# First layer of a two-layer backbone: context tokens in a pass of their own, latents' up projection as seven block products

## The reference

```python
D_MODEL = 1024; SEQ = 1024; CTX_LEN = 256; DEPTH = 2; D_FF = 2816

def _modulate(x, shift, scale):
    return x * (1 + scale) + shift

def _conv_ffn(u, w_up, conv_w, w_down):
    gate, val = jnp.split(_dwconv3(u @ w_up, conv_w), 2, axis=-1)
    return (jax.nn.silu(gate) * val) @ w_down

# per layer, after the first residual h = h + gt1 * mixer(...)
h = h + gt2 * _conv_ffn(_modulate(_rmsnorm(h, norm2[layer]), sh2, sc2), *ffn)
if not last:
    hc = hc + cgt2 * _conv_ffn(_modulate(_rmsnorm(hc, norm2[layer]), csh2, csc2), *ffn)
```

## Time and profile before

| what | value |
|---|---|
| median of 3 runs | 3210.61 us (3210.31 to 3213.64) |
| profiled execution | 3206.37 us |
| its span in the trace | 3204.4 us |
| mean granted clock of TensorE | 0.97 |
| busy: TensorE, VectorE, ACT, POOL | 3016.6, 1765.9, 953.6, 1015.6 us |
| read from and written to HBM | 185.5 MB, 20.8 MB |

### The profile page before, as it was taken

The page is one execution under the profiler, slowest core; times in us unless marked ns, Lnnn a source line. Parts: engine busy times, 40 slices in busy tenths (PEclk is TensorE's granted clock), DMA queues, the critical chain, the costliest instruction groups (busy, mean ns, idle before and its releaser), DMA issues. The chain is left out here.

```text
span 3204.4 us, 67073 instructions
## 1 busy us (share of the span) xinstructions
PE 3016.6 (94%) x28758; PEld 2470.4 (77%) x28758; DVE 1765.9 (55%) x2673; ACT 953.6 (30%) x1800; POOL 1015.6 (32%) x644
## 2 busy tenths in 40 slices
PE   6998999999999999899989889999988899999999
PEld 4655888888888888788867667878767678888887
DVE  4623444555554454722246666777755766666666
ACT  4011221000000000220036566666632433233232
POOL 3212223223333323152311100000004466666664
PEclk9998999999999999999989989999989999999999
DMA  5431011222222221022312011111012111111112
GB/s 236 151 123 37 23 46 46 86 92 92 92 92 92 80 85 40 20 89 81 99 47 63 21 33 29 31 32 34 23 40 92 38 42 66 40 53 66 40 53 79
DMA packets 86541, 210.55 MB, mean 66 GB/s; under 512 B 8434, under 2 KB 44658, under 8 KB 86003
## 3 DMA queue, kind: packets, MB, share of 16 engines
q1 hardware_dynamic: 73442, 157.21, 14.7%
q10 hardware_dynamic: 12816, 49.16, 4.4%
HBM read 185.50 MB, written 20.84 MB: 64 GB/s over the span
## 5 line engine op out<-in xcount | busy, mean ns | idle before, releaser
L155 POOL TENSOR_TENSOR w_hi<-w_raw,zero 128x1024 fp32r<-128x1024 f32 x93 | 177.9, 1913 | 830.0 <-PE ps L167 552.7
L167 PE MATMUL ps<-u_hi,w_hi 128*128 128x512 f32 (+1 forms) x1560 | 395.1, 361 | 3.3 <-DVE ffn_cv L869 2.2
L167 PE MATMUL ps<-u_lo,w_hi 128*128 128x512 f32 (+1 forms) x1560 | 391.4, 358 | 0.0
L167 PE MATMUL ps<-u_hi,w_lo 128*128 128x512 f32 (+1 forms) x1560 | 391.4, 358 | 0.0
L167 PEld LDWEIGHTS ps<-u_hi,w_hi 128*128 128x128 f32 x1560 | 259.6, 188 | 74.2 <-issue 26.6
L167 PEld LDWEIGHTS ps<-u_hi,w_lo 128*128 128x128 f32 x1560 | 259.9, 188 | 46.5
L167 PEld LDWEIGHTS ps<-u_lo,w_hi 128*128 128x128 f32 x1560 | 259.8, 188 | 46.4
L1318 ACT ACTIVATE ffn_cv<-ps,small 128x1280 f32<-128x1280 f32 x44 | 58.6, 1332 | 688.8 <-PE ps L167 680.3
L867 DVE SCALAR_TENSOR_TENSOR ffn_cv<-ps,small,ffn_cv 128x1023 f32<-128x1023 f32 x88 | 77.7, 883 | 307.9 <-ACT ffn_cv L1318 306.4
L158 POOL TENSOR_TENSOR w_lo<-w_raw,w_hi 128x1024 fp32r<-128x1024 f32 x93 | 228.3, 2455 | 7.3
L1697 POOL TENSOR_TENSOR f_w_lo<-h,f_w_hi 128x512 fp32r<-128x512 f32 x92 | 138.4, 1514 | 149.7 <-ACT f_w_hi L1905 149.7
(11 more groups left out here) (443 smaller groups left out, 7040.0 us busy)
## 6 DMA issues: line engine op xcount, KB each, us to landing
w_raw<-in_ffn SPq DMA_DIRECT2D x66, 512.0 KB, 3.4
ada_tile<-in_ada_rows ACTq DMA_DIRECT2D x64, 512.0 KB, 4.0
h<-in_ffn SPq DMA_DIRECT2D x34, 512.0 KB, 4.8
f_w_raw<-in_ffn SPq DMA_DIRECT2D x32, 512.0 KB, 4.0
ada_ring_s<-in_ada SPq DMA_DIRECT2D x22, 512.0 KB, 3.3
w_raw<-in_cd_in SPq DMA_DIRECT2D x20, 512.0 KB, 4.2
z_scratch<-cd_stage ACTq DMA_DIRECT2D x15, 640.0 KB, 5.5
ada_first<-in_ada SPq DMA_DIRECT2D x16, 512.0 KB, 15.5
```

What stands on the lines that cost most here:

```text
L155: pool.tensor_tensor(hi, K.raw[:, raw, :], K.zero[:, 0:1].to_broadcast([P, KT * P]), ALU.add).then_inc(self.hi_done, 1)
L167: mm = pe.matmul(K.ps[:, slot, c, 0:width], wt[:, s, w], x[:, k, at:at + width], start=start and n == 0, stop=stop and n == 2)
```

## The change

`ffn_phase` and `ModRows` go; `split_ffn_phase` with `ThreeWayNorm` and `RowDots` takes their place for layer 0.

- The output projection's chunks are now context first, then latents 0:512 and 512:1024. The norm is written out by ACT and VectorE alone.
- Context pass: 66 blocks (gate f, value f, down f-1) of 24 matmuls with 256 columns, results of the downs summed in PSUM over all f. All FFN weights are loaded for it, and again for the latents. Five raw/lo buffers, three hi buffers. ACT writes hi; POOL writes lo of two blocks in three, VectorE of the third. During f = 1 to 16 VectorE and ACT also form the latents' operand sums (`dve_sums`, 16 quarters).
- Then the context's residual is added, its part of `K.h` is stored in DRAM, and its place in SBUF serves as a buffer for weights and for the row dots; after the last dot it is loaded back.
- Latents: 22 ups of seven products as in layer 1, ten down groups and the end, in the order of ITEMS. Only two buffers hold act_hi, so `rounded` and `low` of a second up come at m = 7 of the down behind it. Two row dots per item, over one tile.
- `InProduct`: the context's squares wait for its h to be back; steps 3 to 7 of chunk 0 come behind the last residual add; order of sums and spreads moved.

Two host arrays change with it: `ada_rows` is now the 48 row tiles once, in order.

```diff
-    STEPS = {(1, 5): [0], (1, 6): [1], (1, 7): [2], (2, 0): [3], (2, 2): [4], (2, 4): [5], (2, 6): [6], (2, 7): [7]}
...
-        if (c, m) in ((1, 1), (2, 4)):
-            self.norm.pe_sums(pe, c - 1)
-        if (c, m) == (1, 4):
+    def pe_between(self, pe, m):
+        if m == 1:
+            self.norm.pe_sums(pe, 0)
+        if m == 4:
             self.norm.pe_spread(pe, 0)
...
                 pe.wait_ge(W.split, m + 1)
+                pe.wait_ge(self.end_added, 2 * KT if c else (KT + 3, KT + 4)[m])
                 for k in range(KT):
                     if m == 0:
                         norm.pe_ready(pe, c, k)
                     mm = product_at(pe, K, m, self.slot(m), K.uhi, K.ulo, k, k, c, at, w, k == 0, k == KT - 1)
+                    if (c, m, k) == (1, 1, 3):
+                        norm.pe_sums(pe, 2)
                 if c == 1:
                     mm.then_inc(self.done, 1)
                 if (c, m) == (0, 0):
+                    norm.pe_sums(pe, 1)
+                if (c, m) == (0, 1):
                     norm.pe_spread(pe, 1)
-                if (c, m) == (0, 1):
-                    norm.pe_sums(pe, 2)
-                if (c, m) == (1, 0):
+                if (c, m) == (1, 1):
                     norm.pe_spread(pe, 2)
...
-        for c in range(3):
+        for c in range(2):
             for m in range(KT):
                 norm.act_square(act, c, m)
-                if (c, m) in ((1, 1), (2, 5)):
-                    norm.act_root(act, c - 1)
+                if (c, m) == (1, 1):
+                    norm.act_root(act, 0)
                 for k in self.STEPS.get((c, m), []):
                     norm.act_hi(act, 0, k)
+        for k in self.LEFT:
+            norm.act_hi(act, 0, k)
+        norm.act_root(act, 1)
         for k in range(KT):
             norm.act_hi(act, 1, k)
+        for m in range(KT):
+            norm.act_square(act, 2, m)
         norm.act_root(act, 2)
         for k in range(KT):
...
+        for k in self.LEFT:
+            norm.dve_step(dve, 0, k)
+        norm.dve_invert(dve, 1)
         for k in range(KT):
             norm.dve_step(dve, 1, k)
+        for m in range(1, KT):
+            norm.dve_acc(dve, 2, m)
         norm.dve_invert(dve, 2)
         for k in range(KT):
...
+class ThreeWayNorm(TokenNorm):
+    CHUNKS = [(1024, 256, 1), (0, 512, 0), (512, 512, 0)]
+    POOL_KS = ()
...
+        elif quarter == 1:
+            dve.wait_ge(self.t1_full, j + 1)
+            dve.scalar_tensor_tensor(self.t2[2][j], tb, self.shift(2, j + HK), self.t1[2][j], ALU.add,
+                                     ALU.subtract).then_inc(self.t2_full, 1)
+            dve.wait_ge(self.b22_hi, j + 1)
+            dve.scalar_tensor_tensor(self.b22[1][j], tb, self.shift(2, j + HK), self.b22[0][j], ALU.add,
+                                     ALU.subtract).then_inc(self.b22_lo, 1)
+            dve.wait_ge(self.t1_hi, j + 1)
+            dve.wait_ge(self.t2_full, j + 1)
+            dve.tensor_tensor(self.t1[1][j], self.t1[2][j], self.t1[0][j], ALU.subtract).then_inc(self.t1_lo, 1)
+        elif quarter == 2:
+            dve.wait_ge(self.t2_full, j + 1)
+            dve.tensor_tensor(self.t3[2][j], self.b11[0][j], self.t2[2][j], ALU.subtract).then_inc(self.t3_part, 1)
+            dve.tensor_tensor(self.t4[2][j], self.b21[0][j], self.t2[2][j], ALU.subtract).then_inc(self.t4_part, 1)
+            dve.wait_ge(self.t3_part, j + 1)
+            dve.tensor_tensor(self.t3[2][j], self.t3[2][j], self.b11[1][j], ALU.add).then_inc(self.t3_full, 1)
+            dve.wait_ge(self.t4_part, j + 1)
+            dve.tensor_tensor(self.t4[2][j], self.t4[2][j], self.b21[1][j], ALU.add).then_inc(self.t4_full, 1)
+        else:
+            dve.wait_ge(self.t4_full, j + 1)
+            for t, hi, lo in ((self.t2, self.t2_hi, self.t2_lo), (self.t3, self.t3_hi, self.t3_lo),
+                              (self.t4, self.t4_hi, self.t4_lo)):
+                dve.wait_ge(hi, j + 1)
+                dve.tensor_tensor(t[1][j], t[2][j], t[0][j], ALU.subtract).then_inc(lo, 1)
...
+    def act_load(self, act, i):
+        t, c = self.of(i)
+        if i:
+            act.wait_ge(self.dots, i)
+        if i in (0, 48):
+            act.dma_start(self.cond, self.K.a["cond_rows"][:, c, :].rearrange("p (a b) -> p a b", a=4)).then_inc(
+                self.cond_in, 16)
+        act.dma_start(self.tile, self.K.a["ada_rows"][t].rearrange("p (a b) -> p a b", a=4)).then_inc(self.tile_in, 16)
...
+        dve.wait_ge(self.tile_in, 16 * (i + 1))
+        dve.scalar_tensor_tensor(self.tile, self.tile, 1.0, self.cond, ALU.mult, ALU.mult,
+                                 accum_out=self.K.mod[:, 1, t, c:c + 1]).then_inc(self.dots, 1)
...
+    C_STEPS = [("gate", 0), ("value", 0)]
+    for f in range(1, FT):
+        C_STEPS += [("gate", f), ("value", f), ("down", f - 1)]
+    C_STEPS += [("down", FT - 1)]
+    LOWS, HIGHS, UPS = 5, 3, 3
...
+    def c_by_dve(n):
+        return n % 3 == 2 and n > 2
...
+    def quarter_at(f):
+        return divmod(f - 1, 4) if 1 <= f <= 4 * HK else None
...
+    ITEMS = [("up", 0), ("up", 1), ("up", 2), ("down", 0)]
+    for g in range(1, G - 2):
+        ITEMS += [("up", 2 * g + 1), ("up", 2 * g + 2), ("down", g)]
+    ITEMS += [("up", FT - 3), ("up", FT - 2), ("up", FT - 1), ("down", G - 2), ("end", G - 1)]
...
+            sp.wait_ge(c_added, KT)
+            sp.dma_start(h_ctx, K.h[:, :, gap]).then_inc(h_out, 16)
+            for unit in ITEMS[3:]:
+                load(unit)
+            sp.wait_ge(rows.dots, rows.DOTS)
+            sp.dma_start(K.h[:, :, gap], h_ctx).then_inc(h_back, 16)
+            sp.wait_ge(prod_done, 7 * FT)
+            nxt.W.load(sp)
...
+                if t == P4:
+                    pe.wait_ge(merged, merges(f, U3))
+                if t == P3:
+                    pe.wait_ge(merged, merges(f, C22))
...
+                    if t == P1 and pending is not None:
+                        centre_gate(pending)
+                    if t == P7:
+                        keep(n)
+                        if pending is not None:
+                            silu(pending)
+                        if n == 0:
+                            act.wait_ge(h_out, 16)
+                        rows.act_load(act, a)
+                    if t == P2:
+                        rows.act_silu(act, a)
+                    if t == P5:
+                        c11(n)
+                        rows.act_load(act, b)
+                    if t == P3:
+                        centre_value(n)
+                        rows.act_silu(act, b)
+                        pending = n
+                else:
+                    if t == 0:
+                        if pending is not None:
+                            centre_gate(pending)
+                        rows.act_load(act, a)
+                    if t == 2:
+                        if pending is not None:
+                            silu(pending)
+                        rows.act_silu(act, a)
+                        pending = None
+                    if t == 3:
+                        rows.act_load(act, b)
+                    if t == 4:
+                        rows.act_silu(act, b)
...
+            def c_step(n):
+                kind, f = C_STEPS[n]
+                if kind == "gate":
+                    c_taps(f, 0)
+                elif kind == "value":
+                    c_taps(f, 1)
+                    dve.wait_ge(c_conv, 2 * f + 2)
+                    dve.wait_ge(c_silu, f + 1)
+                    dve.tensor_tensor(c_value[:, :], c_value[:, :], c_gate[:, :], ALU.mult).then_inc(c_mul, 1)
+                    dve.wait_ge(c_mul, f + 1)
+                    if f >= 2:
+                        dve.wait_ge(c_done, C_NTH["down", f - 2] + 1)
+                    dve.tensor_copy(c_act_hi[f % 2][:, :], c_value[:, :]).then_inc(c_act_hi_done, 1)
+                    dve.wait_ge(c_act_hi_done, f + 1)
+                    dve.tensor_tensor(c_act_lo[f % 2][:, :], c_value[:, :], c_act_hi[f % 2][:, :],
+                                      ALU.subtract).then_inc(c_ready, 1)
+                if n + HIGHS < C_ALL and c_by_dve(n + HIGHS):
+                    i = n + HIGHS
+                    dve.wait_ge(c_hi_done, i + 1)
+                    dve.tensor_tensor(c_lo[i % LOWS][:, :], c_raw[i % LOWS][:, :], c_hi[i % HIGHS][:, :],
+                                      ALU.subtract).then_inc(c_lo_dve, 1)
+                if kind == "value" and quarter_at(f) is not None:
+                    norm.dve_sums(dve, *quarter_at(f))
...
+                if kind == "up":
+                    a, b = dots_in(kind, n)
+                    if pending is not None:
+                        gated(pending)
+                        rounded(pending)
+                    rows.dve_dot(dve, a)
+                    merge(n, U2)
+                    merge(n, U3)
+                    if pending is not None:
+                        low(pending)
+                    merge(n, C22)
```

(24 more changed lines are left out.)

977 lines of the change are left out of this document (648 added, 329 removed).

## The result

Slower, by 1.1%: the median went from 3212.1 us (4 runs beside it) to 3249.8 us (4 runs), ratio 1.011 with a 95% interval of 1.0086 to 1.0133. A later measurement gave 3257.5 against 3219.1, ratio 1.0132 (1.0109 to 1.0156). The profiled execution took 3248.8 us with a span of 3247.0, 42.6 more than the span before.

What follows compares the result with a forecast made beforehand. TensorE, busy 94%, was taken as the bound: -78.0 of matmuls + 3.0 + 1.5 + 19 + 37.6 + 5.9 - 9.3 + 12.5 = -7.8, median 3202.8 us, range 3158 to 3258.

Steps and rivals of the forecast that it cites:

- Rival B: Context pass: VectorE and POOL take turns, 11.8 us per f with a quarter; 3243, or 3263 with clock; chance 0.25.
- Part 1: First layer's FFN loops: matmuls take 829.0 us in place of 907.0, -78.0.
- Part 2: Output projection, context chunk first: TensorE waits for weights from POOL, +3.0; start of the context pass, +1.5.
- Part 3: Context pass: VectorE, held by POOL's operations, takes 10.3 us per f with a quarter; +19 (+4 to +53).
- Part 4: Latents' row dots: twelve ups wait 2.8 us on U3 at P4, 4 for late lo's and hi's, +37.6; up 0 +5.9.
- Part 5: Latents: waits of 2.0 to 3.3 us charged no low clock; 1.7 us each only in a rival.
- Part 6: FFN's end with the next projection's first tile, 41 us, -9.3; then the context's chain up to m=2, +12.5.
- Rival C: Context pass: weights don't come in time; at 150 GB/s +41 in place of +19, 3225; chance 0.07.
- A: Context pass and ups: VectorE's operations fall between POOL's, +4 and 2.0 per up; median 3172; chance 0.26.

Runs made afterwards that it cites:

- e8: Against the changed kernel, POOL writes all weight lo's of the context pass and VectorE none: 3286.4 us, context pass 265.6 for 225.5.
- e3: Against the changed kernel, POOL writes each weight lo of the context pass in four pieces: 3236.7 us, context pass 203.7 for 225.5.
- e4: Against the changed kernel, VectorE writes all weight lo's of the context pass but the first three: 3223.6 us, context pass 196.2 for 225.5.
- e2: Against the changed kernel, only the load of an up's first row dot goes ahead of silu, the dot stays behind `rounded`: 3257.6 us.
- e1: Against the changed kernel, an up's first row dot has its load ahead of silu and goes ahead of gated and rounded: 3223.7 us.
- e6: Changed kernel with nearly all context lo's on VectorE, row dots moved from five ups into downs, first norm spread inside its tile: 3191.1 us.

## Why the prediction was wrong

The forecast was 3202.8 with "faster" at 0.51; the time is 3249.8, inside the range of 3158 to 3258, on the other side of the kernel before. Rival B named it, 3243, or 3263 with the clock, with a chance of 0.25. Its mechanism is what the experiments show; its number is luck. It had 54.5 us against the gain in the context pass with its start, where 33.6 came. Its 3243 has no clock in it, where 20.4 came in the twelve ups, and 3.2 for what stands behind the loops, where 10.9 came.

- **Part 1, right within 3.3 us.** Context matmuls stand 0.120 us apart and those of the ups 0.2267, as forecast. The ten downs take 22.13 us each, not 21.80, so the gain is nearer 74.7 than 78.0.
- **Part 2, near.** +1.6 for +3.0 (a block on POOL takes 4.32 us from start to start in the earlier trace rows, not 4.37, which changes nothing); the context pass started without the 1.5.
- **Part 3, mis-sized: +33.6 with the pass's start, for +20.5.** The term that was wrong is "of which the last five f, without quarters, give back 8". They run at 8.6 us, which is TensorE's own pace; TensorE can't be faster than that, so what it lost in the quarters is lost. The 16 f with a quarter lost 1.9 each where I had 1.7, and the last f's activation added a wait of 2.8 with low clock behind. The 10.3 us that I had for such an f came near the 10.5 measured by luck, twice over. It does not follow from its own terms: VectorE's own work (1.9, 1.2, 1.1 and 2.3) adds up to 6.5 us, not 6.7, and 8 operations x 4.8/8.64 x 1.2 us are 5.3 of hold, capped at 4.8, which makes 11.3 to 11.5. And its reason is wrong: operations do not meet POOL's "at the share that it is busy". ACT writes two hi's right behind the middle tap of value f, which starts POOL's two lo's just as VectorE begins the multiply, so the hold comes in every f and takes in two operations, 2.0 and 2.1 us. B's 11.8 with everything held was too much for that; with a third operation on POOL (e8) it is 12.5. The rule of the Trainium skill ("SBUF — State Buffer", section "SBUF: two separate sides"), whole instructions held and nothing shared, agrees with e3, e4 and e8.
- **Part 4, the number right by luck, the cause wrong.** Twelve waits of 2.8 were forecast, and twelve of 2.7 to 3.2 came in the blocks named. But I had U3 late because the tile lands late. e2 shows that the load is not on the path; `rounded` and the dot, both held by POOL, are. Up 0 waited 4.4 for 4.2. The rest of the latents' lag, 5.3 us beyond waits and clock, looks near the 4 put down for late lo's and hi's, but 3.3 of it are the downs' slower matmuls.
- **Part 5, the step that failed and decided the sign.** "I charge nothing to the twelve": I charged no clock for waits of 2.0 to 3.3 us, from one row in which 2.56 us left it alone. With these 20.4 us alone the sum of -7.8 would have been +12.6, slower. All twelve waits had a stretch of half clock behind them and lost 1.7: 20.4 us of the 42.9 by which the sum of the stretches was off (13.1 are the context pass, 3.1 more in the latents, 7.7 behind them, and -1.4 ahead).
- **Part 6, a third of the truth.** End to the first tile: about 43.8 for 41. From there to m = 2 37.8 for 32.9: the context's sums held by POOL and the spread behind a whole tile were not in the sum.
- **Rival C** is out: in no run did an engine wait for the FFN's weights in the context pass, at up to 175 GB/s over the whole pass. **A** is out as the change stands; e4 shows that its context pass exists (196.2 us, where A had 197.4).

What stays open: why executions of the same code differ by up to 22 us in the phases behind the change, why the downs' matmuls stand 0.2305 us apart where the second layer's take 0.2271, and what would take away the waits of ups 2, 20 and 21, which wasn't tried.

## What to carry to other kernels

Before work is added to VectorE beside POOL, find in the order of the queues which signal starts each, and see whether one event starts both. Here it did, and the hold came in every round: charge it in full then, one of POOL's operations for each of VectorE's with SBUF operands, and charge the low clock behind waits of nearly 3 us as well. Moving POOL's work onto VectorE can then shorten both, even where VectorE is the bound (e4). A filler that waits for nothing (a dot whose tile is there) still costs if it stands in front of an operation with a due time; put it where its engine waits for another.

## What the runs showed of the hardware

- One operation of VectorE per operation of POOL: multiply, CAST and subtract of 128x256 took 2.64, 2.39 and 2.47 us in e8 beside three POOL operations, and 0.42, 0.29 and 0.42 alone. A CAST with one SBUF input is held like the others. Taps that read PSUM kept 0.48 us in all of them.
- The clock has no sharp length of wait here. In the latents it fell to half for 3.4 us, 1.7 us lost, behind waits of 1.83, 1.89, 2.28, 2.52 and all of 2.67 and more, and not behind others of 1.74, 1.80, 2.28, 2.31 and 2.60, nor behind the 2.56 of the earlier trace rows. The wait for the last f of the context pass was 2.76 or 2.77 in eleven executions; low clock came behind it in eight of them and not in e1, e3 and e6. Behind 1.55 us or less I found no fall in the latents of these runs.
